# A sixteen-head attention and two routed expert layers: expert pairs with gate and up in one run and a gated selection; attention with early scores and separate query parts

## The reference, cut to what matters

```
def moba_attention(q, kb, vb, kmean):      # one block of 256 keys: plain causal attention
    s = einsum(q, k) * dh ** -0.5, causal mask
    p = softmax(s);  o = einsum(p, v)      # 16 heads of 64
def shared_kv(x, ...): h = modulate(rmsnorm(x, g), shift, scale); k = h @ w_k; v = h @ w_v
def moba_mixer(h, ...): q = h @ w_q ... @ w_o        # queries from another modulation of x
def moe(h, ...):
    scores = sigmoid(xt @ w_router); 8 of 64 experts a token, out of 4 of 8 groups
    w = scores[chosen] / sum * 2.5
    y = sum over chosen of w * ((silu(xt @ w_gate[e]) * (xt @ w_up[e])) @ w_down[e])
    return y + swiglu(xt, ws_gate, ws_up, ws_down)
```

## Time and profile before

| | |
|---|---|
| median of 3 runs | 3458.31 us (3457.79 to 3465.28) |
| the profiled execution | 3460.53 us, its span 3459.0 us |
| TensorE busy | 3208.7 us (93%) |
| VectorE, ScalarE, GpSimd busy | 1441.7, 1058.0, 219.8 us |
| first expert layer, pairs | about 332 to 1127 us |
| attention | about 1127 to 1316 us |
| second expert layer, pairs | about 1366 to 2163 us |

### The profile page before, as it was taken

The page is one execution under the profiler, slowest core; times in us unless marked ns, Lnnn a source line. Parts: engine busy times, 40 slices in busy tenths (PEclk is TensorE's granted clock), DMA queues, the critical chain, the costliest instruction groups (busy, mean ns, idle before and its releaser), DMA issues.

```text
span 3459.0 us, 43885 instructions
## 1 busy us (share of the span) xinstructions
PE 3208.7 (93%) x18320; PEld 2183.6 (63%) x18320; DVE 1441.7 (42%) x2116; ACT 1058.0 (31%) x1422; POOL 219.8 (6%) x257
## 2 busy tenths in 40 slices
PE   4898999999999877999999999899879999997998
PEld 4876444444444755444444444899768999886798
DVE  5644223333331444221222212555675555567554
ACT  2313222222221443222222221434534343444333
POOL 3000111111110000111111110000000000000000
PEclk9988999999999878999999999999999999998999
DMA  9632768888898412766777888554334555443453
GB/s 268 220 135 98 302 265 332 319 326 306 326 400 323 128 55 114 288 253 257 269 270 278 333 354 320 168 190 158 124 130 163 190 180 183 160 156 122 146 189 110
DMA packets 276659, 770.52 MB, mean 223 GB/s; under 512 B 38418, under 2 KB 189026, under 8 KB 213251
## 3 DMA queue, kind: packets, MB, share of 16 engines
q1 hardware_dynamic: 236016, 715.17, 56.2%
q0 software_dynamic: 28960, 44.86, 3.6%
q10 hardware_dynamic: 11508, 7.98, 0.9%
HBM read 924.08 MB, written 1.05 MB: 267 GB/s over the span
## 4 chain that ended last, share of the span: by engine, by line
PE 86%; DVE 7%; DMA 3%; ACT 3%; issue 1%; DVEq 0%; ACTq 0%; POOLq 0%
PE G L1283 19%; PE U L1303 5%; PE B L1303 5%; PE Y L1076 5%; PE Y L1077 5%; PE Y L1078 5%; PE G L1076 4%; PE U L1076 4%; PE U L1077 4%; PE U L1078 4%; PE G L1077 4%; PE G L1078 4%; PE M L1255 4%; PE M L1256 3%; PE Y L1313 2%; PE Y L1314 2%
## 5 line engine op out<-in xcount | busy, mean ns | idle before, releaser
L1628 DVE TENSOR_TENSOR part_lo<-ring,part_hi 128x2048 fp32r<-128x2048 f32 x240 | 549.3, 2291 | 504.6 <-ACT part_hi L808 502.8
L1283 PE MATMUL G<-wide,gathered 128*64 128x512 f32 x2368 | 724.0, 603 | 0.0
L808 ACT ACTIVATE part_hi<-ring 128x2048 fp32r<-128x2048 f32 x240 | 458.8, 1913 | 501.2 <-PE Y L1078 350.4
L849 ACT ACTIVATE gathered<-M,ada,coef 128x256 f32<-128x256 f32 x384 | 195.9, 560 | 670.4 <-PE M L1256 670.4
L1780 DVE SCALAR_TENSOR_TENSOR swi<-G,slot_gate,swi 128x256 f32<-128x256 f32 x96 | 46.4, 483 | 788.4 <-ACT swi L879 788.4
L1283 PE MATMUL G<-arena,gathered 128*64 128x512 f32 x704 | 334.5, 609 | 0.0
L1283 PEld LDWEIGHTS G<-wide,gathered 128*64 128x64 f32 x2368 | 193.4, 137 | 196.9 <-issue 180.7
L1076 PE MATMUL G<-h_hi,part_hi 128*128 128x256 f32 x1056 | 304.4, 288 | 9.9 <-DVE h_lo L1656 9.8
L1076 PE MATMUL U<-h_hi,part_hi 128*128 128x256 f32 x1056 | 299.7, 284 | 11.8 <-DVE part_lo L1628 11.8
L1077 PE MATMUL G<-h_lo,part_hi 128*128 128x256 f32 x1056 | 301.7, 286 | 0.0
L1078 PE MATMUL G<-h_hi,part_lo 128*128 128x256 f32 x1056 | 301.5, 286 | 0.0
(11 more groups left out here) (363 smaller groups left out, 5196.6 us busy)
## 6 DMA issues: line engine op xcount, KB each, us to landing
ring<-in_ffn_w_up_dram SPq DMA_DIRECT2D x88, 1024.0 KB, 5.3
arena<-in_moe_w_down_dram SPq DMA_DIRECT2D x86, 1024.0 KB
wide<-in_moe_w_gate_dram SPq DMA_DIRECT2D x84, 1024.0 KB
wide<-in_moe_w_up_dram SPq DMA_DIRECT2D x84, 1024.0 KB
arena<-in_moe_w_gate_dram SPq DMA_DIRECT2D x44, 1024.0 KB
arena<-in_moe_w_up_dram SPq DMA_DIRECT2D x44, 1024.0 KB
ring<-in_ffn_w_down_dram SPq DMA_DIRECT2D x44, 1024.0 KB, 4.8
wide<-in_moe_w_down_dram SPq DMA_DIRECT2D x42, 1024.0 KB
```

Of the source, the lines that this page charges most:

```text
L808: eng.activation(part_hi[:, n % SPLIT, :], ring[:, slot, :], ACT.Copy).then_inc(hi_ready, 1)
L849: o = eng.activation(gathered[nb % 2][:, k, :], bank["M"][:, c, :], ACT.Identity, scale=coef_m[:, k:k + 1], bias=shift[:, k:k + 1])
L1283: last = mm(bank["G"][rows], lhsT=gathered[p // 2 % 2][:, k, at:at + SLOTS], rhs=units[tile][:, :, k, :], start=(k == 0), stop=(k == K - 1 ...
L1628: eng.tensor_tensor(part_lo[:, n % SPLIT, :], ring[:, slot, :], part_hi[:, n % SPLIT, :].bitcast(F32), ALU.subtract).then_inc(lo_ready, 1)
```

## The change

**Expert pairs.** `up` of a pair is one run of all eight k (pair 0 excepted, which has the two table fills in it). Both gathers come behind it, the second into bank U in place of M. Two of the three scatters that stood ahead of `late_columns` now come ahead of it. `choose_gated` writes a second selection, 0 or the gate, for one pair; `slot_tables` transposes that and multiplies nothing. `tables_out` takes the gate as the maximum over a row of the table, and the 0/1 table as "greater than 0". `over_tables` moves from pair 1 to pair 0, `choose(1)` behind it. On ScalarE silu comes ahead of the two gathers' emptying.

**Attention.** ScalarE makes all of `h`, then all of `hkv`. Queries have parts of their own, `q_hi` and `q_lo`. The scores of head pairs 0 and 1 are computed behind the last k unit, and their maxima, exponents and normalising stand among the v units. In the loop `scores(pair + 2)` comes ahead of `turn(pair)`, and VectorE has two maxima done in advance. **Gains.** The diagonal and the fill for "gm" move from behind the last unit but one to behind units 18 and 20; `spread_gain` for "at" moves between the second and third split of w_o's rows.

```diff
-        fills = [f"g{nb}_{f}", f"g{nb}_{f + 1}"] if nb < BATCHES else []
-        extra = {0: ["turnw"], 1: ["over"]}.get(p, [])
+        fills = [f"g{nb}_{f}"] if nb < BATCHES else []
+        extra = ["turnw", "over"] if p == 0 else []
...
+        gated_select = [diag, over("gated_select1", "turned_rank", 0, [P, TT, P])]
+        q_hi = over("q_hi", "arena", 10240, [P, K, S], F32R)
+        q_lo = over("q_lo", "arena", 12288, [P, K, S], F32R)
... (ScalarE, experts)
-                    if nb < BATCHES:
-                        gather_out(nb, f)
-                        gather_out(nb, f + 1)
...
                     eng.activation(swi[:, p % 2, :], bank["G"][:, 0, :], ACT.Silu).then_inc(silu_ready, 1)
+                    if nb < BATCHES:
+                        gather_out(nb, f)
+                        gather_out(nb, f + 1, "U")
... (ScalarE, attention)
+                        if f in (8, 9):
+                            exponents(f - 8)
... (TensorE, experts)
                 def slot_tables(p):
-                    eng.wait_ge(select_ready, BATCHES * m + p // 2 + 1)
-                    eng.wait_ge(weights_ready, m + 1)
+                    eng.wait_ge(gated_ready, NP * m + p + 1)
                     wait_free(eng, "M", f"{key}S{p}")
...
                     for t in range(TT):
-                        eng.transpose(Mf[:, 0, t * P:(t + 1) * P], pick_of[:, t, :], ident[:])
-                    for t in range(TT):
-                        for tile, (kind, n) in enumerate(MOE[p]):
...
+                        last = eng.transpose(Mf[:, 0, t * P:(t + 1) * P], gated_select[p % 2][:, t, :], ident[:])
...
-                    if p == 1:
+                    if p == 0:
+                        up(p, (0, 1, 2))
+                        turn_tables()
+                        up(p, (3, 4, 5))
                         over_tables()
-                    up(p, (0, 1, 2))
-                    if p == 0:
-                        turn_tables()
+                        up(p, (6, 7))
+                    else:
+                        up(p, range(K))
                     if nb < BATCHES:
                         gather(nb, f)
-                    up(p, (3, 4, 5))
-                    if nb < BATCHES:
-                        gather(nb, f + 1)
-                    up(p, (6, 7))
+                        gather(nb, f + 1, "U")
+                    if p:
+                        scatter(p - 1, 0, 0)
+                        scatter(p - 1, 0, 1)
... (TensorE, gated MLP)
-                if n == 21:
+                if n == 18:
                     ada_fill("ada_gm")
-                if n == 22:
-                    row_fill("gm")
+                if n == 20:
+                    row_fill("gm", gm_diag)
... (TensorE, attention)
+                    if f == 7:
+                        for part in (0, 4):
+                            wait_pair_drained(eng, "qkv", part)
+                        scores(0)
+                        scores(1)
...
                 for pair in range(PAIRS):
-                    turn(pair)
                     if pair + 2 < PAIRS:
                         scores(pair + 2)
+                    turn(pair)
... (VectorE, experts)
+                def choose_gated(p):
+                    for t in range(TT):
+                        for i, (kind, n) in enumerate(MOE[p]):
+                            at, gate = (rank, wtok) if kind == "base" else (over_rank, over_gate)
+                            o = eng.tensor_scalar(gated_select[p % 2][:, t, SLOTS * i:SLOTS * (i + 1)], slot_at[:],
+                                                  at[:, t, n:n + 1], gate[:, t, n:n + 1], ALU.is_equal, ALU.mult)
+                    o.then_inc(gated_ready, 1)
...
-                    eng.tensor_copy(slot_gate[:, p % 2:p % 2 + 1], Mf[:, 1, 0:1])
-                    eng.tensor_copy(turned_select[:, (2 - 2 * odd + p) % 4, :], Mf[:, 0, :]).then_inc(drained["M"], 1)
+                    eng.tensor_reduce(slot_gate[:, p % 2:p % 2 + 1], Mf[:, 0, :], AX.X, ALU.max)
+                    eng.tensor_scalar(turned_select[:, (2 - 2 * odd + p) % 4, :], Mf[:, 0, :], 0.0, None, ALU.is_gt)\
+                       .then_inc(drained["M"], 1)
... (VectorE, attention)
-                split_h(h, "norm_moe0")
-                next_lo(5)
-                wait_done(eng, b.at["unit", "at"] + 3)
-                split_h(hkv, "norm_moe0")
-                coefficient(3, 3, 10)
-                next_lo(8)
...
+                split_h(h, None, q_hi, q_lo)
+                next_lo(2)
+                split_h(hkv, "norm_moe0")
+                coefficient(3, 3, 10)
+                next_lo(5)
                 maxima(0)
+                next_lo()
                 maxima(1)
-                for pair in range(PAIRS):
+                next_lo()
+                normalise(0)
+                next_lo(2)
+                normalise(1)
+                next_lo()
+                maxima(2)
+                next_lo()
+                maxima(3)
+                for pair in range(2, PAIRS):
                     normalise(pair)
```

More of the change, by code:

```diff
@@ L164, in book_all @@
         b.book("G", key + "pairs", NP)
-        b.own("U", key + "pairs", NP)
+        for p in range(NP):
+            if p // 2 + 1 < BATCHES:
+                b.own("U", f"{key}g{p // 2 + 1}_{2 * (p % 2) + 1}")
+            b.own("U", f"{key}down{p}")
         b.own("B", key + "pairs", NP)
@@ L434, in build @@
         sq_done = sem("sq_done")
+        query_out = sem("query_out")
         rms_ready = sem("rms_ready")
@@ L990, in _ @@
                     for pair in range(PAIRS):
-                        exponents(pair)
+                        if pair >= 2:
+                            exponents(pair)
                         if pair >= 1:
@@ L1087, in up_matmuls, with rows_matmuls @@
                             eng.wait_ge(h_ready, ready + k // 2 + 1)
-                        last = exact(bank[bk][:, c, :], [v[:, k, cs] for v in u], (h_hi[:, k, :], h_lo[:, k, :]),
+                        last = exact(bank[bk][:, c, :], [v[:, k, cs] for v in u], (hi[:, k, :], lo[:, k, :]),
                                      k == 0, k == K - 1)
                 last.then_inc(unit_done, 1)
-            def rows_matmuls(parts, bk, bias=None, ready=None):
+            def rows_matmuls(parts, bk, bias=None, ready=None, h_parts=(h_hi, h_lo)):
+                hi, lo = h_parts
                 u = [view_a(p) for p in parts]
@@ L1836, in experts @@
                 o.then_inc(weights_ready, 1)
+                eng.wait_ge(weights_ready, m + 1)
+                choose_gated(0)
                 wait_done(eng, b.at["unit", key] + 2)
-                choose(1)
                 for p in range(NP):
```

121 lines of the change are left out of this document (68 added, 53 removed).

## The result

The changed kernel takes 3307.78 us (median of four runs, 3303.7 to 3311.0), the kernel before 3458.05 beside it: a ratio of 0.956 (0.954 to 0.958). That is 150 us less. The profiled run took 3311.0 us, with a span of 3309.5.

What follows compares the result with a forecast made beforehand. TensorE, busy 3208.7 of 3459.0 us, was taken as the bound, DMA second. 76.5 + 0.9 + 12.4 - 3 - 14 + 36.4 + 7.5 = 116.7 us less gave 3342 us, range 3320 to 3376.

Steps and rivals of the forecast that it cites:

- the scatter's 0.20: Steady expert pair: first scatter product, now behind a gather, loses 0.12 us of its 0.20 extra (bounds 0 and 0.20).
- what the weights take back: Ends of expert layers: late weight loads near DMA's limit and lower clock give back 14 us, bounds 4 and 35.
- attention: Attention: queries made first, earlier keys' parts, opened softmax loop, early diagonal; 36.4 us less, 20.8 of it the loop.
- the steady pairs: Expert layers: 90 gathering pairs each 0.85 us shorter, 76.5 us; 4 pairs without gather, 0.9 us.
- the late columns and bias rows: Seven pairs with late columns, four with bias row: one scatter over VectorE's copy, 0.3 each subtracted, 3 us (0 to 8).
- the start of the second layer: `choose(1)` moved behind the first tables of an expert layer: about 1.0 us less in each layer.
- Gated MLP: End of the gated MLP: wait of 5.7 us for the diagonal and some 1.8 at lower clock go, 7.5 less.
- first pairs: First pair of each expert layer: 3.9 us less plus 1.0, and 2.6 for the second layer's following `up`; sum 12.4.
- DMA taking back much more: Expert layers: weights come late in middle pairs too, 35 us lost rather than 14, and 15 more; 3378, chance 0.15.
- the ring staying: Attention: softmax loop stays near 5.5 us a pair and early softmax delays a v unit by 5; 3358, chance 0.10.
- the wait on a semaphore as the first products' cost: Expert pairs: first products' cost is a semaphore wait, not change of kind; 29 us less gain, 3371, chance 0.10.
- slower: Expert pairs: ScalarE empties U too late, TensorE stands in every pair; 3526 at 2 us of wait, chance 0.03.

Runs made afterwards that it cites:

- up_split: Changed kernel with `up` in three parts again and the two gathers between them, the second still in bank U; 3374.0 us, ratio 0.975.
- over_order: Changed kernel with the next over block's up weights loaded behind this block's down weights instead of ahead of them; 3303.9 us.
- before_over_order: Kernel before with only the over blocks' load order changed: next gate, this block's down, next up weights; 3436.9 us, ratio 0.993.
- shared_parts: Changed kernel with the parts for queries and keys in one buffer again, keys' parts made behind the fourth q unit; 3317.1 us.
- rest_alone: Kernel before with the changes of attention and gated MLP alone, expert pairs as before; 3406.6 us, ratio 0.986.
- split_and_gates: Changed kernel with `up` in three parts and eight one-column products behind each pair's tables; 3406.0 us.
- experiment 4: What made the landing shorter: the run split_and_gates (3406.0 us) and a table over seven kernels of the last closing packet's delay behind the fifteenth.
- release_down: Changed kernel with the next gate and up weights requested behind the first half of `down`, some 6.0 us later; 3396.8 us, ratio 0.982.

## Why the prediction was right and wrong

**Right: what bounds the kernel, and each mechanism of the pair.** TensorE's own row is the bound, changes of kind cost 0.1 to 0.2 us, `up` in one run of 6.9 to 7.0, one first gather product, no cost between banks, no wait of TensorE for ScalarE in front of `down`. 15.35 was said and 15.29 came; the difference is the scatter's 0.20, of which I took 0.12. Over 90 pairs that is 6 us more gain. "TensorEngine Tiling (Array Packing)" of the Trainium skill (Key Properties) says that a change of tiling mode drains TensorE; the pieces at 0.31 to 0.43 beside 0.12 and 0.23 in the changed kernel and in up_split bear it out in that each change has a price.

**The step that failed: what the weights take back.** The text held the landing of the over blocks' down weights at 15.80 and counted a loss of 14, with bounds of 4 and 35; both bounds had the wrong sign. The lengthened pairs shrank from 17.1 to 7.9 us, a gain of 9.2: an error of 23 in the sum of 116.7, and by far the largest. The 15.80 was taken for a property of the load and of the bandwidth. It was a matter of order and of a tail: of the three MB that q0 had to move two were the next block's, not yet wanted (over_order, before_over_order), and 0.9 to 2.9 us were a tail of a few packets, which all four kernels with the eight one-column products show at these loads, in this order of the queue, and no other kernel with this order by more than 0.4. The change took these products away, and with them the tail, which nobody foresaw; why they make it stays open. My first explanation, the place of the requests, holds in part: asking 2.1 us later moved the three landings by 2.2, 0.4 and 1.2. That DMA is at its limit near the layers' ends was read rightly; that the limit then takes back what the pairs gain was not: in the first layer there was one wait of 1.3 and one of 0.3, and the pairs in the middle of both layers lost nothing.

The spans give 149.5 for the 116.7 of the sum. Of the 33 us between them the weights are 23, attention 9 and the steady pairs 6, less 6 for the late columns and bias rows; what is left is within 1.

**The late columns and bias rows, mis-sized.** 3 us were subtracted; the seven pairs gained 0.17 (17.05 to 16.88) and the next ones 0.82 rather than 0.92, the four bias pairs about 0.2: together some 9 us below the steady rate, where 3 were subtracted and 8 was the bound. The copy of 0.70 has one scatter over it now, and the transposes behind it pay again.

**Attention, right in kind and too small.** 36.4 was said, with 1.0 for the start of the second layer 37.4; 46.7 came. The v units' end to the first product of w_o is 27.9 us (1164.9 to 1192.8): 33.1 was said. The first transposes stand 9.5 behind the v units (9.3 was said), but then a pair costs 3.3, not 4.0: I had summed TensorE's part at the lower clock, and with its waits gone it ran at the full one. That is 5.2. Behind the first product of w_o 10.4 came for 7.3, part of it again the clock (the router's products 4.61 us where the kernel before took 6.72), and that part varies from run to run. The queries first (3.7 for 3.1) and the keys' parts (6.2, and shared_parts gives it back) were right.

**Gated MLP, first pairs.** 8.3 by the first trace for 7.5, 5.4 when undone; the first pairs gave 3.8 and 7.3 from T0 to T1 for 3.9 and 6.5. The pieces listed for the first pair add up to 18.9, not 19.1, which is without weight. In the second layer 3.3 of the 7.3 were credited to the wrong change: rest_alone has them with the old expert pairs (22.65 to 19.34).

**The rivals.** DMA taking back much more, the ring staying, the wait on a semaphore as the first products' cost (0.20 gone at U, up_split shows the change of kind), and slower: none occurred. No rival and no bound let the waits shrink, so nothing of the range reached below 3320. A mechanism with a queue in it can move either way when the spacing of its requests changes, and the gains can then add; this belonged in the range with the sign open.

## What to carry to other kernels

When a load lands late at full bandwidth, look at what its own queue moved between request and landing before calling it a limit: here the load stood behind weights needed later, and one exchange in the order was worth 16 us of pair length in the old kernel and 6 in the new one. Group products by the number of columns that they use, since each change costs 0.1 to 0.2 us here. When waits go, recompute the work behind them at the full clock. Before an explanation rests on one run, look in the traces of the others for what it says: split_and_gates alone would let the tail be laid to the length of the pair, but a run at 15.52 us has it and one at 15.98 has not. And a stretch whose length differs by 5 us between runs of the same code (attention's, 211.1 to 216.2) can't tell of an edit worth 1.

## What the runs showed of the hardware

- Two busy queues shared the DMA engines about evenly: 50.5% and 50.4% in the changed kernel from 1866.7, 55.2% and 46.2% in the kernel before from 2007.4, 424 and 426 GB/s in all. "DMA: Bandwidth & Descriptors" of the Trainium skill (Queues, rings and completion order) has each engine take turns between its queues packet by packet; the even shares agree with it.
- The indirect loads moved their first bytes about 4 us behind their request (asked for at 2001.35 in the kernel before; q0 moved 0.07 MB between 4 and 5 us behind that, and 0.28 MB up to 6 us), with q1 busy.
- A load's end can have a tail in which the last of its sixteen closing packets is late, 0.9 to 2.9 us at the three loads of the table in experiment 4 in the four kernels with the one-column products, at most 0.2 in the three without. "DMA: Bandwidth & Descriptors" of the Trainium skill (Latency and other measured facts) tells of two DMA engines that are usually slower, and ties it, as a guess, to loads of this kind; which engine lagged here no row shows.
- Requests whose rows are all out of bounds move no weights, yet they had to be waited for when they were issued late (18 of the 25 waits in release_down, sixteen of them of 0.3 to 2.8 us).
